# Gate stage reordered and its squares summed on VectorE; the layers' weight splits placed behind each step's work

## The reference

```python
# end of the first block: the gate stage
gate = sigmoid(rms_norm(x, ple_norm_g) @ w_ple_gate)      # 1024 -> 1024
x = x + gate * (p @ w_ple_proj)                           # 256 -> 1024
x = rms_norm(x, final_g)
# each of two layers
h = rms_norm(x, norm_g); proj = h @ w_in                  # q, k, v, z, ga, gb
oa = attention(qa, ka, va) * silu(za)                     # grouped, with rotary positions
ob = neighbourhood_attention(qb, kb, vb) * silu(zb)
mixed = sigmoid(ga) * (oa @ w_o_attn) + sigmoid(gb) * (ob @ w_o_na)
x = x + mixed @ w_out
# and a last rms_norm
```

## Time and profile before

| | us |
|---|---|
| median of 3 runs | 1831.9 (1824.37 to 1835.12) |
| the profiled execution | 1820.89 |
| its span, first to last instruction | 1819.6 |
| PE busy | 1714.9 (94%) |
| DVE busy | 869.4 (48%) |
| ACT busy | 611.5 (34%) |
| mean granted clock of PE | 0.955 |

### The profile page before, as it was taken

The page is one execution under the profiler, slowest core; times in us unless marked ns, Lnnn a source line. Parts: engine busy times, 40 slices in busy tenths (PEclk is TensorE's granted clock), DMA queues, the critical chain, the costliest instruction groups (busy, mean ns, idle before and its releaser), DMA issues. The chain is left out here.

```text
span 1819.6 us, 24493 instructions
## 1 busy us (share of the span) xinstructions
PE 1714.9 (94%) x10253; PEld 1460.1 (80%) x10253; DVE 869.4 (48%) x1544; ACT 611.5 (34%) x1080; POOL 67.7 (4%) x64
## 2 busy tenths in 40 slices
PE   7999889989999997889998998999999998999998
PEld 6887677768888886889987787999978886777876
DVE  6245365556636655644443343436544444244443
ACT  5142154333313335423332332223423333233223
POOL 0000000000000002310000000000010000000000
PEclk9999879989999999999998897999999998799998
DMA  6334200033233323221112001233321202012331
GB/s 180 93 73 93 70 13 21 28 103 93 93 93 93 97 93 88 59 70 47 47 48 47 16 32 40 89 105 105 74 66 47 70 24 59 23 36 70 104 105 46
DMA packets 163118, 125.19 MB, mean 69 GB/s; under 512 B 32176, under 2 KB 159792, under 8 KB 163008
## 3 DMA queue, kind: packets, MB, share of 16 engines
q1 hardware_dynamic: 163008, 123.63, 23.7%
HBM read 121.52 MB, written 2.10 MB: 68 GB/s over the span
## 5 line engine op out<-in xcount | busy, mean ns | idle before, releaser
L570 PE MATMUL bank<-h_hi,w_hi 128*128 128x512 f32 (+2 forms) x920 | 330.7, 379 | 18.4 <-issue 14.1
L526 DVE TENSOR_TENSOR w_lo<-w_raw,w_hi 128x2048 fp32r<-128x2048 f32 (+2 forms) x117 | 243.4, 2080 | 208.2 <-ACT w_hi L517 208.1
L570 PE MATMUL bank<-h_lo,w_hi 128*128 128x512 f32 (+2 forms) x920 | 325.8, 374 | 0.0
L570 PE MATMUL bank<-h_hi,w_lo 128*128 128x512 f32 (+2 forms) x920 | 324.1, 372 | 0.0
L517 ACT ACTIVATE w_hi<-w_raw 128x2048 fp32r<-128x2048 f32 (+2 forms) x117 | 201.2, 1721 | 81.4 <-DMA w_raw<-w_in 36.4
L570 PEld LDWEIGHTS bank<-h_hi,w_hi 128*128 128x128 f32 (+1 forms) x920 | 169.2, 192 | 63.4 <-issue 30.9
L570 PE MATMUL bank<-g_hi,w_hi 128*128 128x264 f32 (+1 forms) x784 | 201.6, 321 | 6.7 <-DVE ple_gate L626 4.6
L570 PE MATMUL bank<-g_lo,w_hi 128*128 128x264 f32 (+1 forms) x784 | 197.5, 316 | 0.0
L570 PE MATMUL bank<-g_hi,w_lo 128*128 128x264 f32 (+1 forms) x784 | 196.8, 315 | 0.0
L570 PEld LDWEIGHTS bank<-h_hi,w_lo 128*128 128x128 f32 (+1 forms) x920 | 168.5, 191 | 31.2
L570 PEld LDWEIGHTS bank<-h_lo,w_hi 128*128 128x128 f32 (+1 forms) x920 | 168.7, 192 | 30.2 <-issue 0.2
(11 more groups left out here) (550 smaller groups left out, 2736.2 us busy)
## 6 DMA issues: line engine op xcount, KB each, us to landing
w_raw<-w_in SPq DMA_DIRECT2D x49, 1024.0 KB, 5.3
w_raw<-w_up SPq DMA_DIRECT2D x32, 512.0 KB, 4.8
w_raw<-w_down SPq DMA_DIRECT2D x8, 1024.0 KB, 5.0
w_raw<-w_out SPq DMA_DIRECT2D x8, 1024.0 KB, 5.0
w_raw<-w_in SPq DMA_DIRECT2D x24, 256.0 KB, 4.5
w_raw<-w_out SPq DMA_DIRECT2D x8, 512.0 KB, 3.5
w_raw<-w_ple_gate SPq DMA_DIRECT2D x4, 1024.0 KB, 5.0
w_raw<-w_o_attn SPq DMA_DIRECT2D x8, 512.0 KB, 3.5
```

The lines of the kernel that those rows point to most:

```text
L526: DV.e.tensor_tensor(wlo[u % RING][:, 0:n], raw[u % RING][:, 0:n], whi[u % RING][:, 0:n].bitcast(F32), ALU.subtract).then_inc(*w_low(u))
L570: ins = PE.e.matmul(out, stationary[a](k), moving[b](k)[i], start=first and n == 0, stop=last and n == 2)
```

## The change

In the gate stage the order of the units becomes gate 0, gate 1, projection, gate 2, gate 3; there are four `gate` buffers in place of two; the high and low parts of p lie in the last two tiles of `G_hi`, `G_lo` in place of the first two; the sums of the squares move from POOL to DVE (`sum_both`); the queues of ACT and DVE are written out anew for this order, with their splits at other places. In `ac_qkv` and `dv_qkv` the splits stand behind the rope work of their step, in `ac_mixed_steps` and `dv_mixed_steps` behind the step's own work; a wait on `m_high` there becomes one on `m_low`. The number of splits, products, copies and transfers is the same.

```diff
@@ program()
-        gate, c = place("ple_gate", [P, 2, S], F32, c)
+        gate, c = place("ple_gate", [P, 4, S], F32, c)
@@ unit plan
-        plan_cols(A["w_ple_gate"], 0, 256)
+        plan_cols(A["w_ple_gate"], 0, 512)
         plan(A["w_ple_proj"], 0, 2, [(0, D)])
-        plan_cols(A["w_ple_gate"], 256, D)
+        plan_cols(A["w_ple_gate"], 512, D)
@@
-        P_in = G_hi, G_lo, lambda k: (h_high.at("p", k), h_low.at("p", k))
+        P_hi, P_lo = G_hi[:, KT - 2:KT, :], G_lo[:, KT - 2:KT, :]
+        P_in = P_hi, P_lo, lambda k: (h_high.at("p", k), h_low.at("p", k))
@@ pe_ple
                     ins.then_inc(*product("meta"))
                     pe_row("ple", [row_2[:, :]])
+                elif q == 1:
                     w = pe_unit()
                     for k in range(KT):
                         b = pe_bank(dense_6, "pp", k)
@@ ac_ple, after gains_made
+            for k in range(4):
+                gate_tanh(k)
             for k in range(KT):
+                ac_copy(pp[:, k, :], bank[:, bank_of["pp", k], :], ("pp", k))
+                if k == 0:
+                    ac_split()
+                elif k % 2 and k > 1:
+                    high(k // 2 - 1)
+                    squares(k // 2 - 1)
+            ac_split()
+            high(3)
+            squares(3)
+            for k in range(4, KT):
                 gate_tanh(k)
-                if k:
-                    squares(k - 1)
-                else:
-                    AC.wait_ge(*product.at("pp", KT - 1))
-                AC.wait_ge(*x_added.at("norm_a", k))
-                ac_high("norm_a", k, S, both_gain[:, k:k + 1], permuted=True)
-                if k == KT - 1:
-                    squares(k)
-                if k > 1 and k % 2:
+                high(k)
+                squares(k)
+                if k % 2:
                     ac_split()
@@ dv_ple
+            def sum_both(k):
+                if k == 0:
+                    return
+                DV.wait_ge(*ple_sq.at(k))
+                DV.wait_ge(*(g_sum.at(k - 1) if k > 1 else ple_sq.at(0)))
+                if k < KT - 1:
+                    DV.e.tensor_tensor(acc[:, 0:S], acc[:, 0:S], sq[k % 2][:, 0:S], ALU.add)
+                    DV.e.tensor_tensor(acc_g[:, 0:S], acc_g[:, 0:S], gain_sq[k % 2][:, :], ALU.add).then_inc(*g_sum(k))
+                    return
...
@@ dv_ple, after the meta tokens' low parts
+            for k in range(2, 4):
+                gated(k)
+            added(0)
+            dv_split()
+            for k in range(1, 4):
                 added(k)
+                low(k - 1)
+                sum_both(k - 1)
             dv_split()
-            low(0)
-            for k in range(2, KT):
-                low(k - 1)
+            low(3)
+            sum_both(3)
+            for k in range(4, KT):
                 gated(k)
                 added(k)
-                if k % 2 == 0 and k > 2:
+                if k > 4:
+                    sum_both(k - 1)
+                low(k)
+                if k == 6:
                     dv_split()
-            low(KT - 1)
...
+            sum_both(KT - 1)
             dv_split()
@@ po_ple
             po_root("ple")
-            for k in range(1, KT - 1):
...
@@ ac_qkv
             for n in range(6):
-                if n % 2:
-                    ac_split()
...
+                if n % 2:
+                    ac_split()
@@ dv_qkv
             dv_layer_row(l)
-            dv_split()
             dv_keys(l)
             dv_split()
             dv_queries(l, 0)
+            dv_split()
             dv_scaled_keys(l)
@@ ac_mixed_steps, gate steps (the output steps likewise)
-                        if j:
-                            ac_split()
                         gs = y.sg[:, 2 * which + j, 0:n]
                         AC.wait_ge(*evac_d.at(*key))
                         AC.e.activation(gs, gs, ACT.Tanh, scale=0.5).then_inc(*mg_tanh(l, q, which, j))
+                        if j:
+                            ac_split()
                         yield
@@ dv_mixed_steps, gate steps (the output steps likewise)
-                        if j:
-                            dv_split()
                         key = ("mg", l, q, which, j)
                         DV.wait_ge(*meta_in.at(l))
                         if q and which == 0:
-                            DV.wait_ge(*m_high.at(l, 2 * q - 2 + j))
+                            DV.wait_ge(*m_low.at(l, 2 * q - 2 + j))
                         dv_scaled(halves(y.sg[:, 2 * which + j, 0:n]), bank_halves(bank_of[key], n), halves(y.row[:, 0:n]), key)
+                        if j:
+                            dv_split()
                         yield
```

More of the change, by code:

```diff
@@ L1827, in ac_ple @@
                 AC.wait_ge(*product.at("p", k))
-                AC.e.activation(G_hi[:, k, 0:S], bank[:, bank_of["p", k], :], ACT.Copy).then_inc(*h_high("p", k))
+                AC.e.activation(P_hi[:, k, 0:S], bank[:, bank_of["p", k], :], ACT.Copy).then_inc(*h_high("p", k))
             ac_row("ple", [row_2[:, :]])
+            ac_split()
             AC.wait_ge(*product.at("meta"))
@@ L1845, in gate_tanh, with high @@
                 AC.wait_ge(*evac_d.at("pg", k // 2, k % 2))
-                AC.e.activation(gate[:, k % 2, :], gate[:, k % 2, :], ACT.Tanh, scale=0.5).then_inc(*pg_tanh(k))
+                AC.e.activation(gate[:, k % 4, :], gate[:, k % 4, :], ACT.Tanh, scale=0.5).then_inc(*pg_tanh(k))
+            def high(k):
+                AC.wait_ge(*x_added.at("norm_a", k))
+                if k == KT - 2:
+                    AC.wait_ge(*product.at("pp", KT - 1))
+                ac_high("norm_a", k, S, both_gain[:, k:k + 1], permuted=True)
             def squares(k):
@@ L1891, in gated @@
-                dv_scaled(gate[:, j, :], bank[:, bank_of["pg", k // 2, j], :], row_2[:, :], ("pg", k // 2, j))
+                if k > 3:
+                    DV.wait_ge(*x_added.at("norm_a", k - 4))
+                dv_scaled(gate[:, k % 4, :], bank[:, bank_of["pg", k // 2, k % 2], :], row_2[:, :], ("pg", k // 2, k % 2))
             def added(k):
-                j = k % 2
+                g = gate[:, k % 4, :]
                 DV.wait_ge(*pg_tanh.at(k))
                 DV.wait_ge(*evac_a.at("pp", k))
-                DV.e.scalar_tensor_tensor(gate[:, j, :], gate[:, j, :], 1.0, pp[:, k, :], ALU.add, ALU.mult).then_inc(*ple_step(k))
+                DV.e.scalar_tensor_tensor(g, g, 1.0, pp[:, k, :], ALU.add, ALU.mult).then_inc(*ple_step(k))
@@ L1934, in po_ple @@
             po_root("ple")
-            for k in range(1, KT - 1):
-                PO.wait_ge(*ple_sq.at(k))
-                PO.wait_ge(*(g_sum.at(k - 1) if k > 1 else ple_sq.at(0)))
-                PO.e.tensor_tensor(acc[:, 0:S], acc[:, 0:S], sq[k % 2][:, 0:S], ALU.add)
-                PO.e.tensor_tensor(acc_g[:, 0:S], acc_g[:, 0:S], gain_sq[k % 2][:, :], ALU.add).then_inc(*g_sum(k))
             PO.close("ple")
```

34 lines of the change are left out of this document (12 added, 22 removed).

## The result

The changed kernel takes 1851.8 us (median, 1849.87 to 1853.35) against 1833.5 us before: ratio 1.0136, 95% interval 1.0097 to 1.0175. It is slower, as forecast, but by more than twice the forecast, and outside its range. The quotient of these two medians is only 1.0100, and the executions listed don't show why the ratio is larger, so the loss is 18 to 25 us here. The profiled execution took 1849.87 us, 28.98 us more than the profiled one before.

A forecast was written before the change was run, and what follows sets the result against it. It took PE (94% busy) to bound the layers and VectorE's queue the gate stage's end. Terms -7.8 + 5.6 + 9.8 + 2.2 - 1.9 = +7.9 us on 1831.9 gave about 1840; the forecast's own range was 1833 to 1847.

The forecast's parts named there:

- the gate stage: VectorE's queue sets its end; PE restarts at about 736.1 instead of 743.85, 7.8 us gained, bounds 2.5 to 10.
- The lows: VectorE's `low` operations (L757) in the gate stage: 1.24 us throughout, instead of 2.08 where one met a GpSimd sum.
- The rule cited there: Gate stage: GpSimd contends with VectorE instructions that have two SBUF inputs, so without its sums lows fall to 1.24 us.
- The rival of long lows: Gate stage: permuted access, not GpSimd, makes lows long; gain 2.5 us instead of 7.8, time 1845; chance 0.06.
- L2772: PE's wait at the attention's end, each layer: 7 to 8 us instead of 2.8 and 2.6; +9.8 us in all.
- The copy: Neighbourhood attention: PE's value matmuls wait about 2.5 us for the turned probabilities' copy; +5.6 us over two layers.
- The steady steps: Mixing steps: gate product weights come late, 0.36 us lost six times in layer b, 0 in layer a; +2.2 us.
- the last step: Last mixing step: its split leaves its place ahead of the last mixed features, where PE waited 1.27 and 1.76; -1.9 us.
- The rival by which the layers' splits hold nobody up: Mixing steps' splits cost PE nothing; only gate stage and last step count, -9.7 us, 1822; chance 0.18.
- The clock term: Whole kernel: effect of PE's clock on the time, taken as 0 between bounds of -3 and +5 us.
- the sum without one: All terms with clock at 0 come to +7.9 us; the attentions' terms in it are +5.6 and +9.8 us.
- The clock rival: New attention stalls drop PE to 1.2 GHz, up to 3.4 us more, twice; time 1847; chance 0.14.

The follow-up runs named there:

- gate_only: Kernel before with the whole gate-stage change and nothing changed in the layers: 1812.6 us, ratio 0.9951 to the kernel before.
- after_again: The changed kernel itself, unaltered, measured a second time against the kernel before: 1853.4 us, ratio 1.0170.
- after_filled_2: Changed kernel with PE's waits ahead of layer a (before the k/v unit's wait) and in the attentions filled with unread matmuls: 1827.6 us, ratio 1.0028 to the kernel before.
- na_only: Kernel before with splits moved behind only in the first four mixing steps (q = 0, first branch), in the neighbourhood attention: 1839.2 us, ratio 1.0088.
- end_only: Kernel before with splits moved behind only in the q = 0, second branch mixing steps (gate product 1, attention's end): 1839.9 us, ratio 1.0071.

## Why the prediction was wrong

**What bounds the kernel, and the gate stage: right.** `gated(7)` was forecast done at 736.0; it ran from 735.87 to 736.55 and PE restarted at 736.92 (forecast 736.1). This execution was 1.7 us late already before the stage, so part of the agreement is luck: the chain started at 697.68 (forecast 695.9) and took 38.9 us instead of 40.1. 7.8 us were forecast, 8.1 measured in the stretch, 8.9 in gate_only. This stretch took 56.2 to 58.3 us in the nine profiled kernels with the old gate stage and 47.8 to 48.2 in the five with the new one unfilled, so 8.1 is the low end of 8 to 10. The lows took 1.27 us on the mean, 1.36 at most, and the new sums 0.68. Groups of VectorE, 699 to 746 us, kernel after:

```profile
L757 DVE SCALAR_TENSOR_TENSOR g_lo<-x_feature_major,both_gains,g_hi 128x512 fp32r<-128x512 f32 x8 | 10.2, 1272 | 2.4 <-ACT g_hi L749 2.2
L1918 DVE TENSOR_TENSOR square_sum<-square_sum,squares 128x512 f32<-128x512 f32 x6 | 4.1, 684 | 0.0
```

The rule cited there on the interfaces that GpSimd and VectorE share (the Trainium skill, GPSIMD Engine Reference, 1. Specifications) holds by these rows: without GpSimd's sums no low takes 2.08 us. The rival of long lows is out.

**The waits in the layers: right.** L2772 7 to 8 us: 7.7 and 7.5. The copy 2.5: 2.3 and 2.2. The mechanism, too: in the kernel after the evacuation starts at 1612.75, VectorE's split at 1616.01 behind ScalarE's, and the copy at 1618.22, 5.47 us behind the evacuation (forecast 5.56).

```profile
1612.75 0.69 DVE L626 TENSOR_TENSOR gates_b<-bank,norm_row_b 128x512 f32<-128x512 f32 x1 [4.79 <-PE bank L570]
1616.01 2.29 DVE L526 TENSOR_TENSOR w_lo<-w_raw,w_hi 128x2048 fp32r<-128x2048 f32 x1 [2.57 <-ACT w_hi L517]
1618.22 0.68 DVE L2998 COPY na_probsT_b<-bank 128x512 f32<-128x512 f32 x1
```

The steady steps cost 2.4 for 2.2, and the last step gave 1.4 in layer b (22.0 to 20.6) and 1.0 in layer a (21.3 to 20.3), 2.4 for 1.9. The rival by which the layers' splits hold nobody up is out.

**The clock: the step that failed.** The prediction wrote "The clock term I take as 0 between bounds of -3 and +5". The runs show a clock term far above that: the two attentions of this pair of executions took 14.5 us more than the sum without one gives, and filling the waits took 25.8 us off the median (after_again to after_filled_2), lows of the kernel before included. The clock rival had the mechanism but the wrong size and the wrong place. It charged 3.4 us, from 13 us at 0.74 behind the gate stage, and twice only, where four waits in the attentions grew or were new. Behind the gate stage half level lasted 6.8 us; behind the 2.2 us wait it lasted 13.7. That the stall was shorter and stood "between matmuls" counted against the rival. Yet beyond its own wait layer b's neighbourhood attention, 40.7 us without a gap at full level, lost most by it: 6.5 us. The view that was not read ahead of the change is the granted clock of exactly the stretches in which waits were forecast (1.00 here, 0.87 in layer a). It would have said how much there was to lose: with PE working through it, a low the length of those in the same trace costs half of itself.

**The base: part of the error.** The median of before was taken from 3 executions. In the four later comparisons, on four chips, it was 1825.4, 1824.2, 1829.8 and 1822.7 us, single executions from 1811.3 to 1842.4, so against these 1831.9 was 2 to 9 us too high a base. That made the miss look smaller than it is.

## What to carry to other kernels

An operation moved behind another engine's work costs what is queued behind it: the forecast from the order of the queues was right to within a microsecond at each place. But where PE is the bound, price a new wait of PE as the wait plus half of the half-level time that may follow it, and read the granted clock of that stretch first: in one at full level a wait of 2.2 us cost 8.7. To tell idle time from clock, fill the wait with matmuls that nobody reads; put them ahead of every wait of that place, or they add to it.

## What the runs showed of the hardware

- The clock is a part of the spread between executions. gate_only ran from 1809.42 us at a mean clock of 0.957 to 1828.97 at 0.946, the same program on the same chip.
- A low in one stretch has a part of its cause in the stretch ahead: in na_only the attention's end of layer b has 13.7 us at half level with the wait of before, where it had 3.4; with the long wait of its own it has 20.3 us in the kernel after, and 10.2 in end_only, which has no new wait ahead.
- Not all lows follow waits. In the kernel before PE is busy without a gap here, at 0.63:

```profile
1545.00:1572.70 27.70, 27.70 (x95) 0.63 0.00 1
```

PE's last wait ahead of these matmuls ended at 1534.16 us. The second of the two lows here, 17.1 us, starts only at 1555.5, behind 6.8 us at full level. What sets those is open, and so is why the times of the filled kernels fell short of, or passed, what their traces showed at the filled places.
